# The last residual sum of a two-block network, made by the store's own DMAs

## What is computed

```
for layer in range(DEPTH_2):
    ...
    h = h + rmsnorm_2(m, g[1])
    u = rmsnorm_2(h, g[2])
    h = h + rmsnorm_2(swiglu(u, ffn_w_gate[layer], ffn_w_up[layer], ffn_w_down[layer]), g[3])
return h
```

## Time and profile before

| | |
|---|---|
| median of 3 runs | 1743.44 us (1743.42 to 1743.95) |
| the profiled execution, its own time | 1746.23 us |
| its span in the profile | 1744.5 us |
| PE busy | 1668.5 us, 96% of the span |
| DVE busy | 912.3 us, 52% |
| POOL busy | 221.7 us, 13% |
| end of the last matmul of `ffo2` to the end of the span | about 18 us |

### The profile page before, as it was taken

The page is one execution under the profiler, slowest core; times in us unless marked ns, Lnnn a source line. Parts: engine busy times, 40 slices in busy tenths (PEclk is TensorE's granted clock), DMA queues, the critical chain, the costliest instruction groups (busy, mean ns, idle before and its releaser), DMA issues.

```text
span 1744.5 us, 22104 instructions
## 1 busy us (share of the span) xinstructions
PE 1668.5 (96%) x8263; PEld 1319.8 (76%) x8263; DVE 912.3 (52%) x1360; ACT 626.8 (36%) x930; POOL 221.7 (13%) x204
## 2 busy tenths in 40 slices
PE   1999899999999999999999999999998999999996
PEld 1756688888888867777776788888887688888885
DVE  6775576444344464666667544444337644444223
ACT  1334344222233253555565333333326333333221
POOL 5000105999000030000000000003000000000000
PEclk9999899999999999999998999999998899999998
DMA  7665034554332132111101322233211222233221
GB/s 281 205 199 173 13 133 134 180 180 169 101 115 88 70 105 85 56 49 37 49 28 46 118 97 97 97 102 106 97 57 49 73 96 96 96 96 123 91 75 48
DMA packets 48587, 179.26 MB, mean 103 GB/s; under 512 B 5968, under 2 KB 6640, under 8 KB 48272
## 3 DMA queue, kind: packets, MB, share of 16 engines
q1 hardware_dynamic: 43600, 162.04, 27.5%
q0 software_dynamic: 3776, 14.78, 2.8%
q10 hardware_dynamic: 1152, 1.66, 0.4%
HBM read 173.04 MB, written 2.10 MB: 100 GB/s over the span
## 4 chain that ended last, share of the span: by engine, by line
PE 70%; issue 22%; DVE 5%; ACT 1%; DMA 1%; ACTq 1%; POOL 0%; POOLq 0%; DVEq 0%; SPq 0%
PE bank L383 15%; PE bank L385 15%; PE bank L384 14%; PE bank L1448 3%; PE bank L1450 2%; PE bank L1449 2%; PE bank L1556 2%; PE bank L1512 2%; PE bank L1531 1%; DVE ada_acc L1990 1%; PE bank L1183 1%; PE bank L1184 1%; PE bank L1185 1%; PE bank L1620 1%; PE bank L454 1%
## 5 line engine op out<-in xcount | busy, mean ns | idle before, releaser
L309 DVE TENSOR_TENSOR w_lo<-raw,w_hi 128x1024 fp32r<-128x1024 f32 (+1 forms) x229 | 313.6, 1370 | 576.1 <-ACT w_hi L305 575.9
L305 ACT ACTIVATE w_hi<-raw 128x1024 fp32r<-128x1024 f32 (+1 forms) x229 | 258.0, 1127 | 571.7 <-PE bank L385 486.1
L383 PE MATMUL bank<-h_hi,w_hi 128*128 128x512 f32 x1136 | 448.5, 395 | 0.5 <-DVE w_lo L309 0.5
L384 PE MATMUL bank<-h_lo,w_hi 128*128 128x512 f32 x1136 | 442.6, 390 | 0.0
L385 PE MATMUL bank<-h_hi,w_lo 128*128 128x512 f32 x1136 | 442.5, 389 | 0.0
L383 PEld LDWEIGHTS bank<-h_hi,w_hi 128*128 128x128 f32 x1136 | 213.5, 188 | 50.5 <-issue 5.4
L384 PEld LDWEIGHTS bank<-h_lo,w_hi 128*128 128x128 f32 x1136 | 213.6, 188 | 45.0 <-issue 1.7
L385 PEld LDWEIGHTS bank<-h_hi,w_lo 128*128 128x128 f32 x1136 | 213.6, 188 | 44.3
L383 PE MATMUL bank<-hid_hi,w_hi 128*128 128x512 f32 x528 | 205.6, 389 | 0.0
L384 PE MATMUL bank<-hid_lo,w_hi 128*128 128x512 f32 x528 | 205.4, 389 | 0.0
L385 PE MATMUL bank<-hid_hi,w_lo 128*128 128x512 f32 x528 | 205.4, 389 | 0.0
(11 more groups left out here) (397 smaller groups left out, 2060.3 us busy)
## 6 DMA issues: line engine op xcount, KB each, us to landing
raw<-in_f2i SPq DMA_DIRECT2D x88, 512.0 KB, 3.2
raw<-in_ffi SPq DMA_DIRECT2D x44, 512.0 KB, 3.3
raw<-in_f2o SPq DMA_DIRECT2D x32, 704.0 KB, 4.1
ada_w<-in_ada_w SPq DMA_DIRECT2D x24, 512.0 KB, 4.3
m_out<-in_ada_w POOLq DMA_DIRECT2D x24, 512.0 KB, 3.7
raw<-in_att_w SPq DMA_DIRECT2D x23, 512.0 KB, 3.3
raw<-in_ffo SPq DMA_DIRECT2D x16, 704.0 KB, 4.1
raw<-in_ada_w SPq DMA_DIRECT2D x16, 512.0 KB, 4.8
```

Of the source, the lines that this page charges most:

```text
L305: nc.scalar.activation(WH[par][:, 0:kc * P], RAW[s][:, 0:kc * P], ACT.Copy).then_inc(whi, count)
L309: nc.vector.tensor_tensor(WL[par][:, 0:kc * P], RAW[s][:, 0:kc * P], WH[par][:, 0:kc * P].bitcast(F32), ALU.subtract).then_inc(wlo, count)
L383: pe_.matmul(bank[:, :], w_h, hi[:, k0 + k, :], start=start and k == 0, stop=False)
L384: pe_.matmul(bank[:, :], w_h, lo[:, k0 + k, :], start=False, stop=False)
```

## The change

The last sum of the residual isn't made on DVE any more. SP stores all of `X` to the output in one DMA of 2 MB, placed in its program between the weight loads of `ffi2` and those of `ffo2`, behind a wait on `xs[3]`. In the tail `dve_last_normed` makes only the products, in place in `M`. GpSimd, after its last power, waits for that store (a semaphore that is done by count 16), then for each product, and issues for each chunk a DMA from `M` to the output that adds to what is there (`accum_op`). GpSimd and SP both wait for the 8 of them to land. Elsewhere, two increments of the attention part now share one semaphore (`f_lx`, waited for at 2 instead of `f_ng` at 1); the instruction that is waited for is the same.

```diff
-        store_done = sem("store_done")
+        store_done, sum_done = sem("residual_stored"), sem("last_term_added_in_store")
...
-        def dve_add_normed(nj_, xs):
+        def dve_last_normed(nj_, xs):
 
             nc.vector.wait_ge(n_rb, nj_.turn)
-
-            def add(k):
-                nc.vector.wait_ge(n_t, nj_.t + k + 1)
-                nc.vector.tensor_tensor(X[:, k, :], X[:, k, :], TMP[:, k % 2, :], ALU.add).then_inc(xs, 1)
             for k in range(C):
-                if k >= 2:
-                    nc.vector.wait_ge(xs, k - 1)
-                nc.vector.tensor_tensor(TMP[:, k % 2, :], M[:, k, :], RB[:, :], ALU.mult).then_inc(n_t, 1)
-                if k >= 1:
-                    add(k - 1)
-            add(C - 1)
+                nc.vector.tensor_tensor(M[:, k, :], M[:, k, :], RB[:, :], ALU.mult).then_inc(xs, 1)
...
             stream_renewed("ffi2", 44)
+            sp.wait_ge(xs[3], C)
+            sp.dma_start(outT[:, :, :], X[:, :, :]).then_inc(store_done, 16)
             stream("ffo2", f2o, KH * P, base=16)
-            for k in range(C):
-                sp.wait_ge(xs[4], k + 1)
-                sp.dma_start(outT[:, k, :], X[:, k, :]).then_inc(store_done, 16)
-            sp.wait_ge(store_done, 16 * C)
+            sp.wait_ge(store_done, 16)
+            sp.wait_ge(sum_done, 16 * C)
...
             pool_rsqrt(nj["r4"])
+            pool.wait_ge(store_done, 16)
+            for k in range(C):
+                pool.wait_ge(xs[4], k + 1)
+                pool.dma_start(outT[:, k, :], M[:, k, :], accum_op=ALU.add).then_inc(sum_done, 16)
+            pool.wait_ge(sum_done, 16 * C)
...
-                    act.wait_ge(f_ng, 1)
+                    act.wait_ge(f_lx, 2)
...
-                                             RQ0[32:32 + 3 * NH, :], ALU.add, ALU.mult).then_inc(f_ng, 1)
+                                             RQ0[32:32 + 3 * NH, :], ALU.add, ALU.mult).then_inc(f_lx, 1)
...
-            dve_add_normed(nj["r4"], xs[4])
+            dve_last_normed(nj["r4"], xs[4])
```

More of the change, by code:

```diff
@@ L277, in build_program @@
         f_hi, f_lo, f_sh = sem("final_lead_hi_ready"), sem("final_lead_lo_ready"), sem("final_shift_halves_ready")
-        f_step, f_bias, f_rq, f_lx, f_ng = (sem("final_lead_" + k) for k in ("step", "bias", "scaled", "forget", "gates"))
+        f_step, f_bias, f_rq, f_lx = (sem("final_lead_" + k) for k in ("step", "bias", "scaled", "gates"))
         class Norm:
```

## The result

The changed kernel takes 1751.42 us (median of 5 runs, 1748.77 to 1752.62) against 1743.44 us before (median of 5 runs, 1741.08 to 1744.90): a ratio of 1.0041, with a 95% interval of 1.0029 to 1.0052. It is slower by 5 to 9 us. The forecast was 1744.5 us with "within 0.2%" as the likeliest case; the time lies 0.1 us under the upper end of the range (1738.5 to 1751.5), outside the 1740.0 to 1747.0 of the likeliest case and in the case that had a chance of 0.27.

A forecast was written before the change was run, and what follows sets the result against it. PE was taken to bound almost all of the run, the DMA engines the changed tail: data from 1733.6, 11.0 us for 8 chunks, 0.45 receipt, 0.45 end, so +1.04 on 1743.44, 1744.5 us; range 1738.5 to 1751.5.

The forecast's parts named there:

- within 0.2%: Whole run: the add takes two passes or near it, 0.82 to 1.69 us a chunk, time 1740.0 to 1747.0; chance 0.56.
- the case that had a chance of 0.27: Whole run slower: adds slower than two passes 0.20, DVE holding up POOL 0.04, PE starved 0.03.
- That the DMA engines become the bound of the tail: Tail: products come every 0.60 us, so chunks queue behind the DMA engines, which take again DVE's 5.5 us.
- r, the time of one chunk: Tail: DMA engines' time for one accumulated chunk, 1.38 us, two passes at 380 GB/s; 8 chunks take 11.0 us.
- The start: Tail: POOL's first issue at 1732.3 after the first product, 1.3 us of lead, data moving at 1733.6.
- The issues: Tail: one DMA issue takes POOL 0.52 to 0.78 us, no bound while a chunk's data takes longer.
- The end: After the last chunk's data: 0.45 us of receipt, then 0.45 us from landing to the end of the span.
- As cheap as a store: Tail: an add costs what a store does, 0.69 us a chunk, time 1739.0; chance 0.17.
- Slower than two passes: Tail: fetching from HBM before write-back loses time; three passes, 2.07 us a chunk, 1750.0; decides from 1.69 us; chance 0.20.
- DVE holds up POOL: Tail: DVE's products hold up POOL's issues, data starts only when products are done, 1748.7; chance 0.04.
- PE starved: Between ffi2 and ffo2: early store of over 20.3 us delays weights; at 24 us PE waits 3.7 us, 1748.1; chance 0.03.
- The sign against two passes: Whole run: a time under 1740 or over 1748 us would mean a chunk's time is not two passes.

The follow-up runs named there:

- e4: The changed kernel, but SP stores the products by plain DMAs and nothing is added (residual left out of the result): tail 8.00 us, ratio 0.9973.
- e7: The kernel before, but GpSimd sums chunks 0 to 3 in SBUF, DVE the other four, SP stores all: tail 11.22 us, ratio 0.9987.
- e3: The changed kernel, but GpSimd's 8 DMAs copy the product over the output and add nothing: tail 12.70 us, ratio 0.9994.
- e11: The changed kernel, but GpSimd's 8 accumulating DMAs add into the residual in SBUF, not the output: tail 18.67 us, ratio 1.0026.
- e12: The kernel before with only the early 2 MB store added, the tail's 8 stores writing over it: tail 12.93 us, ratio 0.9998.
- e8: The kernel before, but chunks 0 and 1 stored early and accumulated by GpSimd's DMAs, which it doesn't wait for: tail 11.51 us, ratio 0.9988.
- e2: The kernel before, but GpSimd also waits at its end for SP's 8 stores: tail 15.52 us, ratio 1.0016.
- e1: The changed kernel, but GpSimd doesn't wait for its 8 accumulating DMAs to land; SP still does: tail 18.23 us, ratio 1.0028.
- e6: The changed kernel, but GpSimd's DMAs are plain copies and GpSimd doesn't wait for them: tail 10.92 us, ratio 0.9988.
- e5: The changed kernel with two accumulating DMAs of 1 MB in place of eight of 256 KB: tail 19.08 us, ratio 1.0034.
- e9: The version with GpSimd summing four chunks, but DVE's products for chunks 4 to 7 go through PSUM: tail 10.13 us, ratio 0.9982.

## Why the prediction was right or wrong

- **That the DMA engines become the bound of the tail: right.** DVE gave back 5.6 us (products end at 4.87 us, 4.89 in the sum), and the DMA engines took more than that.
- **r, the time of one chunk: the settled rate right, the size too small.** Two passes at 380 GB/s would be 190 GB/s; the rate settles at 202, or 1.30 us a chunk, where 1.38 was taken. That it is a second fetch fits, and isn't shown. But the first 6 us run at about 150 GB/s, so that data takes 12.7 us in place of 8r = 11.0, or 1.59 us a chunk. That is 1.7 us of the error. The Trainium skill's ratio of 1.93 ("Collectives: The Full Stack", Part 3), measured there between collectives that copy and collectives that add, would have been as near: at full rate e4's stores and this kernel's adds stand at some 380 to 202, or 1.9.
- **The start: 0.4 us too early.** Data begins at 2.5 us of the tail, where 1733.6 - 1731.54 = 2.1 was taken. The lead was right (1.2 us from issue to data, 1.3 taken); GpSimd's first issue was late. It starts 0.6 us behind the end of the first product, where the 0.1 us at which GpSimd's power had followed DVE's mean was taken. In e7 GpSimd's first sum follows its product by 0.1 us; the 0.6 come with its DMAs (e3 has them too).
- **The issues: mis-sized, without effect.** 0.90 us each and not 0.52 to 0.78; the data is slower still, at 1.30 us a chunk and more, and in e11 equally slow issues kept 180 GB/s going from the start.
- **The end: the step that failed, and the largest part of the error.** The sum put the same 0.45 us behind the last landing as the earlier trace rows show when SP is the last engine at work. With GpSimd as the last it is 3.7 us: 3.3 us, half of the loss and more than half of the 5.5 us by which the forecast was short, for which the prediction had no term. It had named no place where GpSimd's new waits at the end are paid; "nothing is queued behind these waits but the end" was true, and the end was what cost.
- The terms together: 1.0 (forecast) + 1.7 + 0.4 + 3.3, and 0.1 of receipt, are the 6.5 us measured.
- **That the time is inside the range is luck.** The range reached to 1751.5 us to make room for adds slower than two passes. What filled that room was mostly the end, which no case held.
- **The rivals.** "As cheap as a store" is out (e3 against after: 6.8 us between the tails). "Slower than two passes" gave about the right time, 1750.0 at three passes, for the wrong reason: the rate settles at that of two, and the 1.59 us a chunk on average are under the 1.69 from which that case was to decide. Its mechanism, a fetch from HBM that loses time, may be in the slow first 6 us, which e11 doesn't have. "DVE holds up POOL" is out: GpSimd's first issue starts 0.6 us behind the end of the first product, while DVE still multiplies, and e3's issues beside the same products take 0.54 us. "PE starved" is out (e12).
- **What would show it.** The sign against two passes was a time over 1748 us; it came, at 1751.4, and the rate is that of two passes all the same. That sign read the time as if r alone could move it. The times to landing grow from 4.3 to 10.6 us, 0.9 a DMA, between the 0.7 of two passes and the 1.1 named for the slow case. The sign that a wait on DVE no longer ends last held; the page's chain ends in GpSimd's DMAs.

## What to carry to other kernels

A sum that is moved into the store's DMA isn't free: in these runs the data moved at about half the rate of a plain store. It paid where the DMA had time to spare, and not at the end of the program, where its latency and its bytes were all on the path (e8 against the changed kernel). Ask which engine will be the last to leave: on these runs GpSimd's last wait cost 2.6 us more than SP's. Where GpSimd is idle in a tail, let it compute in SBUF beside a DVE that takes its second operand from PSUM, and leave the last stores to SP.

## What the runs showed of the hardware

- With GpSimd waiting for the last landing the program ended 3.0 us behind it (e2), or 3.7 us where it had issued the DMAs too (the changed kernel, e3); with SP alone it was 0.45 us (before). When the DMAs that land last were issued by GpSimd, the end came 1.4 us later even when it doesn't wait for them (e1 and e6, 1.6 us of SP's wait against 0.2). Why that is so stays open; the trace has no row for it.
- Accumulating DMAs of 256 KB settled at some 200 GB/s from SBUF to HBM and ran at some 185 within SBUF, where plain ones ran at some 380 from SP (e4) and mostly 335 to 400 from GpSimd (e3); the first lands after 4.3 us (HBM) or 3.5 us (SBUF), a plain one from GpSimd after 2.4 and one from SP after 2.0.
- Eight accumulating DMAs of 256 KB ran at about 150 GB/s for their first 6 us; two of 1 MB didn't (e5), nor did eight of 256 KB within SBUF (e11). The cause wasn't settled.
- A DVE sum of 128x512 with both operands in SBUF took up to 1.44 us beside GpSimd's sums (e7), and 0.68 us with one operand in PSUM (e9).
